# Attention in a two-block transformer kernel: probabilities scaled in the step of their scores, transposes one step behind

## The reference, cut to what matters

```python
logits = einsum('bqhd,bshd->bhqs', qb, k) * scale + bias_or_mask
p = softmax(logits, axis=-1)
out = einsum('bhqs,bshd->bqhd', p, v)
```

## Time and profile before

| | |
|---|---|
| Median of 3 runs | 3686.38 us (3681.68 to 3692.76) |
| Profiled execution, own time | 3688.7 us |
| Its span in the trace | 3686.9 us |
| TensorE busy | 3470.0 us, 94% of the span |
| VectorE busy | 2220.9 us, 60% |
| ScalarE busy | 599.5 us, 16% |
| Mean granted TensorE clock | 0.973 of full speed |
| Hybrid attention, 8 pairs | 585.6 to 847.9 us |
| MLA attention, 4 pairs | 1820.1 to 1947.3 us |
| Dilated attention, 3 pairs | 2491.4 to 2687.2 us |

### The profile page before, as it was taken

One profiled execution on the slowest core, in us unless ns is written; L12 is line 12 of the kernel. 1 busy time (PEld: TensorE's weight loads), 2 busy tenths in 40 slices (PEclk: granted clock), 3 DMA queues, 4 the chain that ended last, 5 costly groups with the idle time before them and its releaser, 6 DMA issues.

```text
span 3686.9 us, 40877 instructions
## 1 busy us (share of the span) xinstructions
PE 3470.0 (94%) x16392; PEld 2869.3 (78%) x16392; DVE 2220.9 (60%) x4309; ACT 599.5 (16%) x1244; POOL 12.8 (0%) x12
## 2 busy tenths in 40 slices
PE   4999989888999999999888999989899999999998
PEld 3888867667888888888657888867678875888887
DVE  7665657766765766654636554553436567587754
ACT  1000012232000010000231000013321134012110
POOL 0000000000000000000000000010000000000000
PEclk9999989998999999999999999999999999999999
DMA  5642511111442534332101222222212211222222
GB/s 210 210 148 92 208 61 46 47 46 56 159 140 104 196 112 151 126 109 95 51 35 58 90 82 89 83 76 76 70 58 85 87 64 46 80 80 90 82 86 75
DMA packets 61797, 355.67 MB, mean 96 GB/s; under 512 B 6261, under 2 KB 14965, under 8 KB 32117
## 3 DMA queue, kind: packets, MB, share of 16 engines
q1 hardware_dynamic: 61607, 353.05, 27.4%
HBM read 350.77 MB, written 9.34 MB: 98 GB/s over the span
## 4 chain that ended last, share of the span: by engine, by line
PE 88%; DVE 7%; issue 3%; ACT 1%; DMA 1%; DVEq 0%; SPq 0%; ACTq 0%
PE turn L400 38%; PE lin L400 29%; PE lin L347 5%; PE lin L438 5%; PE score L1224 2%; PE turn L347 1%; PE out L1209 1%; PE lin L435 1%; PE turn L1194 1%; DVE work L756 1%; DVE normed_sums L529 1%; DVE work L670 1%; PE out L770 1%; PE out L400 1%; PE turn L438 1%
## 5 line engine op out<-in xcount | busy, mean ns | idle before, releaser
L400 PE MATMUL turn<-normed_sums,weight_ring 128*128 128x256 f32 x3880 | 915.7, 382 | 0.0
L400 PEld LDWEIGHTS turn<-normed_sums,weight_ring 128*128 128x128 f32 x3880 | 743.1, 192 | 103.3 <-issue 0.5
L400 PE MATMUL lin<-normed_T,weight_ring 128*128 128x256 f32 x2176 | 508.4, 385 | 48.4 <-ACT normed_T L709 26.0
L400 PEld LDWEIGHTS lin<-normed_T,weight_ring 128*128 128x128 f32 x2176 | 415.8, 193 | 110.4 <-issue 46.6
L465 DVE TENSOR_TENSOR products<-products,lin 128x512 f32<-128x512 f32 x188 | 129.1, 687 | 526.9 <-PE lin L400 496.2
L400 PE MATMUL turn<-arena,weight_ring 128*128 128x256 f32 x1650 | 379.1, 379 | 2.7 <-DVE arena L529 2.7
L400 PE MATMUL lin<-arena,weight_ring 128*128 128x256 f32 x1576 | 365.8, 385 | 1.9 <-DVE arena L2593 1.0
L400 PEld LDWEIGHTS turn<-arena,weight_ring 128*128 128x128 f32 x1650 | 313.1, 190 | 46.7 <-DVE arena L529 2.1
L400 PEld LDWEIGHTS lin<-arena,weight_ring 128*128 128x128 f32 x1576 | 302.8, 193 | 44.9 <-issue 1.8
L400 PE MATMUL lin<-normed_sums,weight_ring 128*128 128x256 f32 x1312 | 322.6, 383 | 6.0 <-DVE normed_sums L529 6.0
L400 PEld LDWEIGHTS lin<-normed_sums,weight_ring 128*128 128x128 f32 x1312 | 250.1, 191 | 45.4 <-issue 8.0
(11 more groups left out here) (289 smaller groups left out, 3413.3 us busy)
## 6 DMA issues: line engine op xcount, KB each, us to landing
weight_ring<-in_up SPq DMA_DIRECT2D x110, 1024.0 KB, 4.8
weight_ring<-in_down SPq DMA_DIRECT2D x40, 1024.0 KB, 4.9
arena<-in_ada SPq DMA_DIRECT2D x48, 768.0 KB, 4.4
normed_T<-in_ada SPq DMA_DIRECT2D x42, 768.0 KB, 5.0
weight_ring<-in_down SPq DMA_DIRECT2D x20, 768.0 KB, 4.2
weight_ring<-in_dil_qk SPq DMA_DIRECT2D x9, 1024.0 KB, 4.9
weight_ring<-in_hyb_qk SPq DMA_DIRECT2D x8, 1024.0 KB, 4.8
weight_ring<-in_xbc SPq DMA_DIRECT2D x6, 1024.0 KB, 4.8
```

What stands on the lines that cost most here:

```text
L400: last = pe.matmul(o[:, n * H:(n + 1) * H], weight_block(slot, pairs, block, kp), op(kind, kp0 + kp), start=opens and n == 0 and kp == kps ...
```

## The change

Three things change, all in the attention helpers, so in all three stages:

- VectorE scales a unit's probabilities in the step in which the unit's last scores were made. It waits there for ScalarE's exponentials of that same step, and only then goes on to the step's fill.
- The lag falls from 2 to 1 (`by_unit`) and from 3 to 2 (`by_part`), so that transposes follow their scores by one step, or two.
- A pair takes 6 steps instead of 7, and 11 instead of 12 in the dilated stage. The same fill is spread over them.

```diff
-        by_unit = Heads(2, (2, 3, 4, 5))
-        by_part = Heads(3, (2, 3, 4, 5, 0, 1, 8, 9))
-        STEPS, DIL_STEPS = QT + 3, 2 * RES + 4
+        by_unit = Heads(1, (2, 3, 4, 5))
+        by_part = Heads(2, (2, 3, 4, 5, 0, 1, 8, 9))
+        STEPS, DIL_STEPS = QT + 2, 2 * RES + 3
...
-                if 0 < t <= len(order) and order[t - 1][1] == len(units[order[t - 1][0]]["parts"]) - 1:
-                    n, q = order[t - 1]
-                    st = stat[:, (unit0 + n) % 4, :]
-                    parts = units[n]["parts"]
-                    v.wait_ge(probs_ready, 2 * (pair0 + t))
+                if t < len(order) and order[t][1] == len(units[order[t][0]]["parts"]) - 1:
+                    v.wait_ge(probs_ready, 2 * (pair0 + t + 1))
                     if q == 1:
                         vlink(v, c, v.tensor_tensor(st[:, 6:8], st[:, 6:8], st[:, 8:10], ALU.add))
                     vlink(v, c, v.reciprocal(st[:, 10:12], st[:, 6:8]))
                     for p, part in enumerate(parts):
                         for hh in range(2):
-                            probs = kind.logits(2 * (pair0 + t - len(parts) + p) + hh)[:, 0:part["n"]]
+                            probs = kind.logits(2 * (pair0 + t + 1 - len(parts) + p) + hh)[:, 0:part["n"]]
                             v.tensor_scalar(probs, probs, st[:, 10 + hh:11 + hh], None, ALU.mult).then_inc(probs_normed, 1)
```

## The result

The changed kernel is slower: ratio 1.0175 (95% interval 1.0153 to 1.0196). The medians are 3750.9 us (3749.4 to 3758.3, 4 runs) and 3688.7 us for the kernel before on the same chip, so +62 us; forecast were +51 and 3737 us, range 3703 to 3770. The profiled execution is the longest of the four, 3758.3 us with a span of 3756.6, so its trace shows 7.5 us more than the median does; its mean clock is 0.965, that of the other three 0.969 or 0.970.

A forecast was written before the change was run, and what follows sets the result against it. TensorE was taken to bound full pairs, the chain of scores, softmax and transposes the bare ones, VectorE nearly hybrid pair 1. Terms 15 + 17 + 10 + 3 + 6 = +51 us gave 3737 us, range 3703 to 3770.

The forecast's parts named there:

- The price of the wait: VectorE's wait for same-step exponentials: transposes start 2.1 to 3.8 us after scores, 12.0 us per four-step pair.
- Bare pairs, +15: Pairs without fill: uncovered round trips add 5 us each to MLA pair 3, hybrid pair 7, dilated pair 2.
- I take the middle, +5: Dilated pair 2: 22 us against 13.7 idle, some slow TensorE work beside VectorE's; ends +0.5 and +9, +5 taken.
- Dilated pairs 0 and 1, +17: Moved group borders make TensorE wait for banks in steps 1, 5 and 7: 2.5, 3.3, 2.9 us, 8.7 a pair.
- Hybrid pairs 0 to 6, +10: VectorE's held queue: pairs 1 and 4 +3 each, pairs 0, 2, 5 and 6 +1 each, pair 3 unchanged.
- MLA pairs 0 to 2, +3: Fill nearly covers the trips; steps 2 and 3 lack 0.5 and 1.1 us, so +1 us a pair.
- The clock, +6: TensorE matmuls slowed after about eight new pauses of 2.3 us and more, each costing nothing or 1.7 us; half taken.
- Clock collapse: Rival: pauses keep the clock low in dilated pairs 0 and 1, falling to 0.8; 3775 us; chance 0.13.
- Only the bare pairs: Rival: dilated bank waits are bridged and hybrid pairs keep pace, +15 and a few, 3703 us; chance 0.12.
- Faster: Rival: transposes find probabilities ready and pairs drain sooner; half of 26.0 us of TensorE waits goes, 3673 us; chance 0.07.

The follow-up runs named there:

- experiment 10: The changed kernel plus matmuls whose result nobody reads, filling TensorE's waits in the three bare pairs: 3738.6 us, ratio 1.0132.
- 12: Kernel before with fill over 6 and 11 steps, hybrid and MLA scaling at the next step's head, unread matmuls in bare pairs: 3651.2 us, 0.9890.
- Experiment 8: The changed kernel with dilated pairs kept at 12 steps and their old group borders: 3738.1 us, ratio 1.0136.
- experiment 4: The change applied to the kernel before in the hybrid and MLA stages only, dilated stage as before: 3719.7 us, ratio 1.0093.
- experiment 1: Kernel before with only the scaling moved into the step of its scores, old lags and steps: 3713.3 us, ratio 1.0070.
- Experiments 2: Kernel before with only its fill spread over 6 and 11 steps, old lags and scaling: 3666.7 us, ratio 0.9944.
- 11: The changed kernel (short lags, same-step scaling) with the old 7 and 12 steps and old fill spread: 3763.5 us, ratio 1.0200.
- experiment 5: The changed kernel with its fill over 5 of 6 and 10 of 11 steps, last step empty: 3736.4 us, ratio 1.0133.

## Why the prediction was right, and by how much

The direction, the mechanism and the size hold: +62 against +51, inside the range. Point by point:

- **The price of the wait.** Right. 12.6 us of round trips in a bare pair against 12.0, 4.74 against 4.8 in the dilated unit.
- **Bare pairs, +15.** Mis-sized: +6.2, +6.1 and +11.1, together 23.4. The sums of idle time were right: hybrid pair 7, MLA pair 3 and dilated pair 2 idle 13.9, 13.7 and 22.3 us by the windows, against the forecast's 13.7, 13.2 and 22. The step that failed is "I take the middle, +5" for dilated pair 2, which took off some 4 us for slow matmuls that lie beside VectorE's work. Nothing came off: the idle time grew by 8.6 us, from 13.7 to 22.3. On top, TensorE's busy time in the three pairs grew by 1.0, 0.6 and 2.5 us for the same matmuls, which no term but the clock's allowed for. With the clock up (experiment 10) the pairs are 0.5, 1.7 and 2.7 us longer than before, but the slow matmuls were there before the change as well: on the old lags, 12 gets 7.0 us out of the same three pairs. Of the 11.1 of dilated pair 2, 7.2 remain with the clock up on both sides.
- **Dilated pairs 0 and 1, +17.** The waits stand in the steps read from the order, 8.1 and 8.0 us a pair against 8.7. Pair lengths grew by 10.3 and 11.7: waits and the clock behind them. Experiment 8 takes both away by moving group borders alone (80.0 and 79.8).
- **Hybrid pairs 0 to 6, +10.** Right where the clock held: in experiment 4 pairs 1 and 3 took 34.5 and 34.3 against 33.8 and 34.5. Pair 4 took 45.3 (forecast 43.6) and 43.7 in 4, but pair 2 43.2 there (forecast 41.6). All seven grew by 17.9 in the changed kernel's profile, by 10.6 in 4's and as much in those of 8 and 10.
- **MLA pairs 0 to 2, +3.** Measured 1.3, 3.1 and 1.4; the clock is 0.95 in pair 1 and 1.00 in the other two.
- **The clock, +6.** Too little; it is the other mis-sized term. The page splits the 69.7 us of the profiled execution into 44.7 of idle time and 25.0 of slower matmuls, while my terms other than the clock add up to 45. The agreement is rougher than it looks, as those terms are lengths of pairs and hold a little of the clock.
- **The rivals.** Clock collapse didn't come: dilated pair 0 has 0.98. "Only the bare pairs" falls with the 16.1 us of bank waits. "Faster" described a real effect: in experiment 1 the wait for the scaling falls from 26.0 to 8.1 us. It was paid for by VectorE's queue, as the forecast had it, and in the change the short lag took even that away.
- **What the forecast did not see.** It took the edit of the steps for the same jobs in other groups. Experiments 2 and 11 against the change show that it is worth some 20 us on the old lags and some 10 on the short ones. On the short ones that is a gain of some 24 us in the hybrid and MLA stages (11 against 8), less the 13 that the dilated borders cost (the change against 8). The change is thus a gain and two larger losses, the wait (+28) and the lags (+45), and my sum hit the total without knowing the gain. In part that is luck: the terms were priced for the 6 and 11 steps, so the gain went into them unseen.

The steps of experiments 1, 11 and the change are one order of taking the edits apart; in another order the shares would differ. What remains open is why the clock of a pair differs between executions (below).

## What to carry to other kernels

When an engine's instruction waits for a round trip to another engine, price what stands behind it in its queue, not the wait: here, in experiment 1, the waits for the scaling fell by 18 us and the kernel still lost 28. Shorten a software pipeline only where the fill of one step is longer than the round trip; let the fill of a phase end one step before the phase does, so that its last combination is covered (some 20 us here on the old lags; with VectorE's new wait in place, experiment 5, the hybrid stage grew by it). A second empty step gave the gain back. Where a chain of round trips leaves TensorE idle in every step, check the granted clock first: matmuls nobody reads took 18.6 us out of three such pairs, and 12 out of the whole.

## What the runs showed of the hardware

The same instructions behind like pauses got different clocks in different executions. Hybrid pair 1 in the changed kernel (TensorE, the pause and what followed it):

```profile
635.70 0.95 PE L1194 MATMUL turn<-constants,work 128*128 128x128 f32 x4 [1.90 <-DVE work L1266]
636.59 0.70 PE L1209 MATMUL out<-work,arena 128*64 128x128 f32 x4
637.21 3.23 PE L1224 MATMUL score<-arena 64*128 64x384 f32 x8
640.37 3.78 PE L438 MATMUL lin<-normed_sums,weight_ring 128*128 128x256 f32 x8
```

The same pair in experiment 4, where TensorE's work and order in it are the same:

```profile
634.78 0.70 PE L1194 MATMUL turn<-constants,work 128*128 128x128 f32 x4 [1.82 <-DVE work L1252]
635.41 0.44 PE L1209 MATMUL out<-work,arena 128*64 128x128 f32 x4
635.78 1.76 PE L1224 MATMUL score<-arena 64*128 64x384 f32 x8
637.48 1.99 PE L438 MATMUL lin<-normed_sums,weight_ring 128*128 128x256 f32 x8
```

Eight matmuls of 384 columns take 3.23 or 1.76 us, eight of the fill 3.78 or 1.99: the clock is at 1.2 GHz in the first case, at 2.4 in the second, behind pauses of 1.90 and 1.82 us. The pair took 37.1 and 34.5 us. The same shows within one execution, the changed kernel's. In dilated pair 0 the pause of 3.04 us was followed by eight matmuls at full speed, 1.99 us; in dilated pair 1 the same pause in the same place was followed by this, and in experiment 10, pair 0, the eight took 3.78 us:

```profile
2656.85 3.55 PE L438 MATMUL lin<-normed_T,weight_ring 128*128 128x256 f32 x8 [3.04 <-DVE products L478]
```

The pause of 2.77 us was followed by eight transposes at 1.62 in pair 0 and at 1.91 in pair 1. The length of the pause alone doesn't decide. The Trainium skill, page "TensorE: Matmul & The Clock Gate", section "Loop structure matters more than you think", says that VectorE's copy out of PSUM doesn't break the warmth of matmuls that follow immediately. Here they don't follow immediately, since TensorE waits for that emptying, and behind such waits both clocks were seen, at 3.04 us even in the same place. The same page of the Trainium skill, section "A second HAM failure mode: psum-queue depth-cycling", says that brief idling again and again between groups makes the clock swing, and the bare pairs agree: their mean granted clock is 0.51, 0.80 and 0.74 with the waits, 0.93, 1.00 and 1.00 with them filled.
